# A sparse-attention mixer: the indexer's projections first, relevance on halves of the array, tile 0's sums first

## The reference, cut to what matters

```
def dsa_mixer(h, w_in, cq_g, ckv_g, w_uq, w_uk, w_uv):
    cq, ckv, qi, ki, wi = jnp.split(h @ w_in, C_SPLITS, axis=-1)    # widths 384, 256, 8*64, 64, 8
    q = (rmsnorm(cq, cq_g) @ w_uq).reshape(b, s, C_HEADS, C_NOPE)
    ckv = rmsnorm(ckv, ckv_g)
    q_lat = jnp.einsum('bshd,hcd->bshc', q, w_uk)
    ...
    for i0 in range(0, s, Q_BLOCK):                                 # two tiles of 128 queries
        rel = jax.nn.relu(jnp.einsum('bthd,bsd->bths', qi[:, i0:end], ki[:, :end]))
        score = jnp.einsum('bths,bth->bts', rel, wi[:, i0:end]).astype(jnp.float32)
        _, idx = lax.top_k(jnp.where(admissible, score, -jnp.inf), kk)      # kk = 64
        c_sel = jax.vmap(lambda c, i: c[i])(ckv[:, :end], idx)
        logits = jnp.einsum('bthc,btkc->bthk', q_lat[:, i0:end], c_sel).astype(jnp.float32) * scale
        ...
```

## Time and profile before

| what | value |
|---|---|
| median of three runs | 1085.67 us |
| the profiled execution, its own time | 1085.41 us |
| its span, first to last instruction | 1083.7 us |
| TensorE busy | 1070.7 us, 99% of the span |
| DVE busy, ACT busy | 776.0 us (72%), 564.6 us (52%) |
| 748 to 845 us: TensorE, DVE, ACT busy | 96.4, 69.9, 58.8 of 97.0 us |
| granted TensorE clock, mean | 0.999 |
| DMA | 194.59 MB, mean 180 GB/s |

### The profile page before, as it was taken

One profiled execution on the slowest core, in us unless ns is written; L12 is line 12 of the kernel. 1 busy time (PEld: TensorE's weight loads), 2 busy tenths in 40 slices (PEclk: granted clock), 3 DMA queues, 4 the chain that ended last, 5 costly groups with the idle time before them and its releaser, 6 DMA issues.

```text
span 1083.7 us, 16043 instructions
## 1 busy us (share of the span) xinstructions
PE 1070.7 (99%) x6172; PEld 938.9 (87%) x6172; DVE 776.0 (72%) x1015; ACT 564.6 (52%) x816; POOL 67.8 (6%) x169
## 2 busy tenths in 40 slices
PE   8999999999999999999999999999999999999997
PEld 7888888998889888888888888888978989888886
DVE  5966769875886786676778667678487768676675
ACT  6534446667766753443465344345466666443442
POOL 3000010110020200000010000002100101000000
PEclk9999999999999999999999999999999999999999
DMA  8756474564144365644536564453804435745641
GB/s 322 249 192 222 165 273 132 170 205 151 50 184 152 108 247 199 228 166 183 194 108 246 209 233 159 190 194 108 272 14 143 175 117 195 252 159 191 222 165 40
DMA packets 50155, 194.59 MB, mean 180 GB/s; under 512 B 4496, under 2 KB 24480, under 8 KB 31792
## 3 DMA queue, kind: packets, MB, share of 16 engines
q1 hardware_dynamic: 48832, 189.54, 49.2%
q0 software_dynamic: 1264, 4.25, 1.4%
HBM read 192.73 MB, written 1.05 MB: 179 GB/s over the span
## 4 chain that ended last, share of the span: by engine, by line
PE 91%; DVE 5%; ACT 2%; issue 1%; DMA 1%; POOL 0%; SPq 0%; POOLq 0%; ACTq 0%; DVEq 0%
PE psum L960 21%; PE psum L1076 21%; PE psum L968 11%; PE psum L941 5%; PE psum L1061 3%; PE psum L1298 3%; PE psum L946 3%; PE psum L784 2%; PE psum L786 2%; PE psum L785 2%; PE psum L980 1%; PE psum L1267 1%; PE psum L1168 1%; PE psum L810 1%; PE psum L811 1%; PE psum L809 1%
## 5 line engine op out<-in xcount | busy, mean ns | idle before, releaser
L2322 DVE TENSOR_TENSOR w_ring<-raw,w_ring 128x2048 fp32r<-128x2048 f32 (+2 forms) x120 | 272.8, 2273 | 25.4 <-ACT w_ring L1656 25.1
L1656 ACT ACTIVATE w_ring<-raw 128x2048 fp32r<-128x2048 f32 x121 | 230.7, 1907 | 47.3 <-DMA raw<-in_ffn_w_gate 25.3
L2439 DVE TENSOR_REDUCE work<-psum 128x256 f32<-128x512 f32 x172 | 114.4, 687 | 175.3 <-PE psum L968 161.2
L960 PE MATMUL psum<-h_both,w_ring 128*128 128x512 f32 x1024 | 237.3, 389 | 0.0
L960 PEld LDWEIGHTS psum<-h_both,w_ring 128*128 128x128 f32 x1024 | 192.2, 188 | 39.9
L1076 PE MATMUL psum<-w_ring,g_both 128*128 128x512 f32 x936 | 220.0, 390 | 0.0
L1076 PEld LDWEIGHTS psum<-w_ring,g_both 128*128 128x128 f32 x936 | 173.2, 188 | 34.3
L1754 ACT ACTIVATE V<-work 128x512 f32<-128x512 f32 x44 | 27.9, 634 | 249.3 <-DVE work L2448 249.3
L968 PEld LDWEIGHTS psum<-h_both,w_ring 128*128 128x128 f32 x1024 | 127.1, 192 | 2.5
L968 PE MATMUL psum<-h_both,w_ring 128*128 128x256 f32 x1024 | 127.9, 283 | 0.0
L2322 DVE TENSOR_TENSOR w_ring<-QT,w_ring 128x2048 fp32r<-128x2048 f32 x40 | 91.4, 2285 | 2.4 <-ACT w_ring L1656 2.4
(11 more groups left out here) (336 smaller groups left out, 1560.7 us busy)
## 6 DMA issues: line engine op xcount, KB each, us to landing
raw<-in_ffn_w_gate SPq DMA_DIRECT2D x43, 1024.0 KB, 4.8
raw<-in_ffn_w_up SPq DMA_DIRECT2D x43, 1024.0 KB, 4.8
QT<-in_ffn_w_down SPq DMA_DIRECT2D x40, 1024.0 KB, 4.8
raw<-in_ab_w_in SPq DMA_DIRECT2D x7, 1024.0 KB, 5.5
gain_row<-in_norm_g POOLq DMA_DIRECT2D x8, 512.0 KB, 6.6
raw<-in_ffn_w_down SPq DMA_DIRECT2D x4, 1024.0 KB, 4.7
raw<-in_xa_wk SPq DMA_DIRECT2D x4, 1024.0 KB, 4.8
raw<-in_ab_w_out SPq DMA_DIRECT2D x4, 1024.0 KB, 5.0
```

Of the source, the lines that this page charges most:

```text
L960: nc.tensor.matmul(outs[-1][:, :], hi[:, k, P * j:P * (j + 1)], h_both[:, k].rearrange("p a n -> p (a n)"), start=(k == 0), stop=False)
L1656: nc.scalar.activation(w_hi[:, c % RING, 0:k * n], raw_at(c)[:, 0:k * n], ACT.Copy)\
L2322: nc.vector.tensor_tensor(w_lo[:, c % RING, 0:k * n], raw_at(c)[:, 0:k * n], w_hi[:, c % RING, 0:k * n].bitcast(F32), ALU.subtract).then_i ...
L2439: nc.vector.tensor_reduce(dst[:, p % 2, TOK * j:TOK * (j + 1)], bank(name).rearrange("p (a n) -> p n a", a=2), AX.X, ALU.add)\
```

## The change

Five things change in stage 5, and nothing elsewhere:

1. The chunks are cut and ordered anew: c.2 (the last 128 columns of the query latents, the keys and the head weights), c.0, qi.0, qi.1, and last c.1 (the key-value latents alone). `mixer_begin` takes c.2 and c.0.
2. The keys are scaled into both halves of one row, with no zeros, and two transposes instead of four make one `kiT`, in which both halves of the rows hold the 64 keys. A relevance product takes 64 rows: the head in rows 0 to 63 into one bank, the head in rows 64 to 127 into another. `head_of` gives the head that stands in each place. A call of `relevance(t, m)` on TensorE is four products for two banks.
3. c.1 is projected tile by tile between the relevance products, and its copies and squares follow on ACT.
4. Tile 0's four sums come before tile 1's. DVE does five of tile 0's eight rounds, two of tile 1's sums, the scaling of the key-value latents, the last three rounds, the mask, and two sums more.
5. queries(1) stands before cckvT's transposes and keys(0), instead of after keys(0).

```diff
-C_COLS = [("c.0", (0, 256)), ("c.1", (256, 512)), ("c.2", (512, 640), (1152, 1224)), ("qi.0", (640, 896)),
-          ("qi.1", (896, 1152))]
+C_COLS = [("c.2", (256, 384), (1152, 1224)), ("c.0", (0, 256)), ("qi.0", (640, 896)), ("qi.1", (896, 1152)),
+          ("c.1", (384, 640))]
...
+def head_of(i, j):
+
+    return 4 * (i // 2) + i % 2 + 2 * j
+
+
+RELEVANCE = [(t, i) for t in range(NT) for i in range(4)]
...
-    rel0.0 rel0.1 rel1.0 rel1.1 ccqT.0 ccqT.1 cckvT rel0.2 rel0.3 cuq.0.0 rel1.2 rel1.3 cuk.0 cuq.0.1
+    rel0.0 rel0.1 c.1.0 rel0.2 rel0.3 c.1.1 rel1.0 rel1.1 ccqT.0 ccqT.1 cuq.0.0 rel1.2 rel1.3 cuq.0.1 cckvT cuk.0
...
-LAST_USE = {"ua": "mk.1", "uqn": "uqn.1", "ukv": "v.1", "ca": "cuq.1.1", "cb": "cuv.1.1"}
+LAST_USE = {"c.1": "c.1.1", "ua": "mk.1", "uqn": "uqn.1", "ukv": "v.1", "ca": "cuq.1.1", "cb": "cuv.1.1"}
...
-            mixer_begin(5, ["c.0", "c.1"])
-            token_major("c.2", h_hi, h_lo)
+            mixer_begin(5, ["c.2", "c.0"])
+            pe.wait_ge(ki_done, 1)
+            transposes("kiT", [kk2[:, t, 0:P] for t in range(NT)])
             feature_major("qi.0", h_hi, h_lo)
-            pe.wait_ge(ki_done, 1)
-            transposes("kiT", [kk2[:, t, P * j:P * (j + 1)] for j in range(2) for t in range(NT)])
-
-            def relevance(t, i):
+
+            def relevance(t, m):
                 n = P * (t + 1)
-                up(f"rel{t}.{i}", [(slice(TOK * j, TOK * j + n),
-                                    [(qiT[:, i, P * t:P * (t + 1)], kiT[:, j, 0:n])]) for j in range(2)])
+                outs = [take(f"rel{t}.{2 * m + j}") for j in range(2)]
+                for i in range(2):
+                    for j in range(2):
+                        o = slice(64 * j, 64 * (j + 1))
+                        last = nc.tensor.matmul(outs[j][:, TOK * i:TOK * i + n], qiT[o, 2 * m + i, P * t:P * (t + 1)],
+                                                kiT[o, 0, 0:n], start=True, stop=True)
+                        if i:
+                            filled(f"rel{t}.{2 * m + j}", last)
...
             relevance(0, 0)
+            filled("qi.1", feature_terms(out_[:, TOK:2 * TOK], hi, lo, h_hi, h_lo, 1))
+
+            def key_value_latent(t):
+                hi, lo = weights(C["c.1"])
+                filled(f"c.1.{t}", token_terms(take(f"c.1.{t}")[:, 0:256], hi, lo, h_hi, h_lo, t))
+
+            key_value_latent(0)
+            ready("qi.1")
             relevance(0, 1)
-            filled("qi.1", feature_terms(out_[:, TOK:2 * TOK], hi, lo, h_hi, h_lo, 1))
+            key_value_latent(1)
             relevance(1, 0)
-            relevance(1, 1)
             pe.wait_ge(lat_done, 3)
             transposes("ccqT.0", [lat[:, t, P * k:P * (k + 1)] for k in (0, 1) for t in range(NT)])
             transposes("ccqT.1", [lat[:, t, P * 2:P * 3] for t in range(NT)])
-            pe.wait_ge(lat_done, 4)
-            transposes("cckvT", [lat[:, t, QL + P * k:QL + P * (k + 1)] for k in (0, 1) for t in range(NT)])
...
-            relevance(0, 2)
-            relevance(0, 3)
             ready("ccqT.0")
             ready("ccqT.1")
             queries(0)
-            relevance(1, 2)
-            relevance(1, 3)
+            relevance(1, 1)
+            queries(1)
+            pe.wait_ge(lat_done, 4)
+            transposes("cckvT", [lat[:, t, QL + P * k:QL + P * (k + 1)] for k in (0, 1) for t in range(NT)])
             ready("cckvT")
             keys(0)
-            queries(1)
             sparse_scores(0)
...
-            for i in range(2):
-                split_to(C[f"c.{i}"] + 2)
-                evacuate(f"c.{i}", lat[:, :, 256 * i:256 * (i + 1)],
-                         bank(f"c.{i}").rearrange("p (t n) -> p t n", t=NT))
-            split_to(C["c.2"] + 2)
-            act.wait_ge(*freed["c.1"])
+            split_to(C["qi.1"])
+            evacuate("c.0", lat[:, :, 0:256], bank("c.0").rearrange("p (t n) -> p t n", t=NT))
+            act.wait_ge(*freed["c.0"])
             act.wait_ge(*freed["c.2"])
-            for name, a, b in (("ccq", 0, QL), ("cckv", QL, QL + KVL)):
-                for t in range(NT):
-                    square(name, t, lat[:, t, a:b])
+            for t in range(NT):
+                square("ccq", t, lat[:, t, 0:QL])
+            split_to(C["c.1"])
+
+            def key_value_latent(t):
+                evacuate(f"c.1.{t}", lat[:, t, QL:QL + KVL], bank(f"c.1.{t}")[:, 0:KVL])
+                act.wait_ge(*freed[f"c.1.{t}"])
+                square("cckv", t, lat[:, t, QL:QL + KVL])
...
+            evacuate("kiT", kiT[:, 0, :], bank("kiT")[:, 0:TOK])
             indexer(0)
-            evacuate("kiT", kiT[:, :, :].rearrange("p h n -> p (h n)"))
             relevance(0, 0)
             relevance(0, 1)
             indexer(1)
+            key_value_latent(0)
+            relevance(0, 2)
+            relevance(0, 3)
+            key_value_latent(1)
             relevance(1, 0)
             relevance(1, 1)
...
+            latent_rows("ccqT.0", 0, 2)
+            latent_rows("ccqT.1", 2, 1)
...
-            relevance(0, 2)
-            relevance(0, 3)
             queries(0)
             relevance(1, 2)
             relevance(1, 3)
+            queries(1)
+            latent_rows("cckvT", 3, 2)
             keys(0)
             split_to(C["co.0"])
-            queries(1)
             keys(1)
...
-            for i in range(3):
-                split_to(C[f"c.{i}"] + 2)
-
+            split_to(C["qi.0"])
             dve.wait_ge(*full("c.2"))
             b = bank("c.2").rearrange("p (t n) -> p t n", t=NT)
-            nc.vector.tensor_copy(lat[:, :, 512:640], b[:, :, 0:128])
-            nc.vector.memset(kk2[:, :, 64:192], 0.0)
+            nc.vector.tensor_copy(lat[:, :, 256:384], b[:, :, 0:128])
             n = norm_no["pre5"]
             for t in range(NT):
                 dve.wait_ge(rstd_done[t], n + 1)
-                for o in (0, 192):
+                for o in (0, 64):
...
+            split_to(C["qi.1"])
+            latent("ccq", 0, QL)
+            split_to(C["c.1"])
...
-            for t, i in RELEVANCE:
-                relevance(t, i)
-            top_rounds(0, range(rounds))
+            for i in range(4):
+                relevance(0, i)
+            top_rounds(0, range(5))
+            relevance(1, 0)
+            relevance(1, 1)
+            latent("cckv", QL, QL + KVL)
+            top_rounds(0, range(5, rounds))
             top_mask(0)
+            relevance(1, 2)
+            relevance(1, 3)
```

More of the change, by code:

```diff
@@ L186, in bank_uses @@
     fill(5)
-    names("c.0 c.1 c.2 qi.0 kiT qi.1")
+    names("c.2 c.0 kiT qi.0 qi.1")
     out.extend(SPARSE.format(*units_of("dsa")).split())
@@ L2045, in _, with latent_rows @@
             ffn(4)
-            for i in range(2):
-                split_to(C[f"c.{i}"] + 2)
-                evacuate(f"c.{i}", lat[:, :, 256 * i:256 * (i + 1)],
-                         bank(f"c.{i}").rearrange("p (t n) -> p t n", t=NT))
-            split_to(C["c.2"] + 2)
-            act.wait_ge(*freed["c.1"])
-            act.wait_ge(*freed["c.2"])
-            for name, a, b in (("ccq", 0, QL), ("cckv", QL, QL + KVL)):
-                for t in range(NT):
-                    square(name, t, lat[:, t, a:b])
+            split_to(C["qi.1"])
+            evacuate("c.0", lat[:, :, 0:256], bank("c.0").rearrange("p (t n) -> p t n", t=NT))
+            act.wait_ge(*freed["c.0"])
+            act.wait_ge(*freed["c.2"])
+            for t in range(NT):
[5 more added lines that the diff above has]
+                square("cckv", t, lat[:, t, QL:QL + KVL])
+            def latent_rows(name, k, n):
+                act.wait_ge(*full(name))
+                for j in range(n):
+                    ins = nc.scalar.activation(latT[:, k + j, :], bank(name)[:, TOK * j:TOK * (j + 1)], ACT.Copy,
+                                               scale=pcol[:, CCQ + k + j:CCQ + k + j + 1])
+                ins.then_inc(freed[name][0], 1)
             def indexer(i):
@@ L2072, in _ @@
             indexer(1)
+            key_value_latent(0)
+            relevance(0, 2)
+            relevance(0, 3)
+            key_value_latent(1)
             relevance(1, 0)
             relevance(1, 1)
-            for name, k in (("ccqT.0", 0), ("ccqT.1", 2), ("cckvT", 3)):
-                n = 1 if name == "ccqT.1" else 2
-                act.wait_ge(*full(name))
-                for j in range(n):
-                    ins = nc.scalar.activation(latT[:, k + j, :], bank(name)[:, TOK * j:TOK * (j + 1)], ACT.Copy,
-                                               scale=pcol[:, CCQ + k + j:CCQ + k + j + 1])
-                ins.then_inc(freed[name][0], 1)
+            latent_rows("ccqT.0", 0, 2)
+            latent_rows("ccqT.1", 2, 1)
             def queries(p):
@@ L2744, in _, with latent @@
             dve.wait_ge(ki_done, 1)
-            for name, a, b in (("ccq", 0, QL), ("cckv", QL, QL + KVL)):
+            def latent(name, a, b):
                 for t in range(NT):
```

10 lines of the change are left out of this document (4 added, 6 removed).

## The result

| kernel | median, us | runs | against the kernel before |
|---|---|---|---|
| before | 1085.78 | 20 | |
| changed | 1087.92 | 20 | 1.0021, 95% interval 1.0014 to 1.0028 |
| changed, second comparison | 1087.55 | 11 | 1.0007, 0.9998 to 1.0016 |
| changed, third comparison | 1087.82 | 11 | 1.0022, 1.0012 to 1.0031 |

The forecast was 1087.3. The first result lies 0.6 us above it and inside its range of 1086.1 to 1088.2. By the three ratios together, weighted by their intervals, the changed kernel is 1.0017 of the one before, 1.8 us slower. The forecast was 1.65 us.

What follows compares the result with a forecast made beforehand. TensorE, 91% of the span, was taken as the bound. The stage's +0.10 us and 1.55 us of switches made +1.65; on the profiled 1085.41 that is 1087.06, and 0.26 to the median gave 1087.3, range 1086.1 to 1088.2.

Steps and rivals of the forecast that it cites:

- Level start: Start of the stage: the shorter first chunk's 0.2 us is lost and the next chunk still starts at 752.02 us.
- Row halves: Relevance products: opposite halves of the array overlap fully, blocks take 0.43 and 0.86 us, and 2.6 us go.
- Rival A: Relevance blocks: the halves take turns without overlap, 2.6 us more, +4.2 in all, 1089.9 us; chance 0.13.
- rival B: Relevance blocks: records start in strict order, five slots instead of four, 0.65 us more, 1088.0 us; chance 0.10.
- Switches: Four relevance blocks: each pays one entry into and one exit from the row-half mode, 1.8 us added.
- e + x: Switch cost at a relevance block: entry e of 0.20 us (between 0 and 0.39) plus exit x of 0.25 us.
- Rival D: Relevance blocks: switches cost nothing, so +0.1 to +0.4 us, about 1085.9 us, no change; chance 0.10.
- Three waits: TensorE idles for ACT's copies before queries(0), keys(0) and the first scores: 1.5, 1.1 and 0.9 us, 3.5 added.
- After this point: From the first probability transposes on: both orders are alike, TensorE stays dense, and nothing takes the lag back.
- DVE: Tile 0's sums end near 779 us and its mask near 788; two TensorE waits on DVE go, 0.7 us.
- rival C: First relevance block: the fifth chunk (c.1) comes late, block 1.9 us late, +3.6, 1089.3 us; chance 0.05.
- E: Faster: switches free and the three waits only a third as long, -2.2 us, 1083.4 us; chance 0.06.

Runs made afterwards that it cites:

- e4: The changed kernel with both products of the lower row half ahead of both of the upper one in each relevance block; 1087.56 us, ratio 1.0016.
- e2: The changed kernel with zero-padded relevance products over all 128 rows instead of row halves; 1088.64 us, ratio 1.0027.
- e3: The changed kernel with the same TensorE products reordered so that other work covers all three handoffs; 1084.11 and 1083.94 us, ratios 0.9987 and 0.9985.
- e6: e1 with the four transposes of the first query latents put ahead of the first tile 1 block; 1085.77 us, ratio 0.9996.
- e7: e3 with whole-height zero-padded relevance products instead of row halves; 1085.68 us, ratio 0.9995.
- e1: The kernel before with only the relevance products on row halves (one form of the keys, two transposes); 1086.67 us, ratio 1.0010.

## Why the prediction was right

| step | before | forecast | after, less 0.47 |
|---|---|---|---|
| key transposes | | 760.55 | 760.53 |
| third block | | 779.8 | 779.78 |
| queries(0) | | 783.3 | 783.28 |
| keys(0) | | 791.3 | 791.38 |
| first probability transposes | 799.22 | 800.87 | 801.11 |

- **Level start**: right. The first chunk's 0.2 us is lost at the transposes of x; the next chunk stands at 752.02.
- **Row halves**: full overlap, 2.6 us, as taken. Rival A is refuted by the block lengths (1.07 and 0.64 us, where turns would take 1.72 and 0.87 and the switches on top), rival B by the same lengths and by e4.
- **Switches**: e + x was put at 0.45 us. From the rows: the last product before a block starts at 769.74 and the block would be due at 769.86, so the block is 0.09 late. From its start to the next product are 0.64, 0.21 over the four slots. The product after that comes 0.22 later, 0.10 over its pitch. That is 0.40 for both. The tile 1 blocks take 1.07, also 0.21 over. That this is the halves' and not the place's is shown by e2: its whole-height blocks, at the same places behind the same work, start on pitch, take 0.81 and 1.73 us and are followed on pitch. Rival D is refuted. The forecast of 1.55 us for the four blocks was about 0.15 too high.
- **Three waits**: 1.5, 1.1 and 0.9 were forecast; 1.56, 0.98 and 0.73 are marked. The forecast counts by pitch, and a bracket begins only at the end of the last record, which is later. By pitch the first is 781.32 + 0.65 to 783.75 = 1.78, the second 790.27 + 0.44 to 791.85 = 1.14, the third 791.85 + 1.72 to 794.58 = 1.01 us: 3.9 in sum where 3.5 was forecast. The first is the longer because TensorE was done sooner, the switch being cheaper than forecast. ACT's copies set its end, and from the block's start to queries(0) are 3.50 us against 3.47 forecast. So the forecast had the switches too dear and the waits too short, and the two partly cancel. With a few hundredths at keys(0) and in the products behind, the last row of the table is 0.24 later than forecast.
- **After this point**: right, as far as the traces can tell. I had written that nothing takes the lag back. Between the two traces 1.89 becomes 1.67, but that is mostly the 0.17 us stretch at 828.10, which in e3 comes and goes with the execution. Nor does being later decide it: counted from 739 us, e6 reaches that place level with the kernel before (within 0.02 us) and e7 0.2 us sooner, and neither has the stop. So 1.67 against 1.65 is nearer than the forecast deserves: it was 0.24 short at the last row of the table, and one stop in one trace of the kernel before hides most of that.
- **DVE**: tile 0's sums ended at 779.45 and its mask was written at 787.83 (less the 0.47: 778.98 and 787.36; forecast: near 779 and near 788). The losses of 0.44 and 0.28 us in the earlier trace rows are gone, and TensorE had nothing more to gain from it.
- **c.1's chunk (rival C)**: its ACT part started at 764.76, where 764.1 and the 0.47 make 764.6. The block was not late.
- **E**: the handoffs are not shorter than taken.

Timeline of DVE, changed kernel, the mask of tile 0:

```profile
779.49 0.29 DVE L2788 MAX8 top<-vaug 128x8 f32<-128x128 f32 x1
...
787.83 0.23 DVE L2793 TENSOR_SCALAR xmT<-vaug 128x128 f32<-128x128 f32 x1
```

Change or no change: the forecast called 0.2% the edge and gave 0.60 to "no change" and 0.35 to slower. The first result, 1.0021 with 1.0014 to 1.0028 around it, lies on that edge, so which side it fell on is luck. The miss of size is 0.6 us in the time, of which about 0.15 is the stage's (1.8 by the three ratios in place of 1.65) and 0.1 the kernel before (1085.78 for 1085.67). The rest is within the scatter of a comparison: 1.0007 to 1.0022 for one kernel.

One cost the prediction never looked at: a block asks for both its banks before its first product. In the changed kernel other work stands ahead of each block (24 to 72 products, or queries(0)), its banks were free, and this had no price. In e1 it cost 1.37 us. That the prediction wasn't hurt by it was not its doing.

## What to carry to other kernels

Before moving a piece away from between two others, write down which copy it covered. Here three handoffs TensorE to ACT to TensorE, each about 0.2 us and the copies queued on ACT, left TensorE idle for 3.3 us when uncovered, more than the 2.6 us of array time saved. Once work stood over them again, the same savings made the kernel 0.14% faster than before. Packing products onto row halves also makes one block ask for two banks at the same time: count when the second bank comes free, not only the first.

## What the runs showed of the hardware

- Products of 64 rows on opposite row halves run side by side in full: eight fp32 records of 256 columns in four slots of 0.215 us, and the starts of a pair are 7 ns apart (13 ns where both products of one half come first in the program). The order in the program within the block doesn't matter for this (e4).
- Going from whole-height products to row halves and back costs 0.35 to 0.40 us for both ways together, in blocks of 0.64 and of 1.07 us. Whole-height blocks at the same places (e2) have no such cost.
- Ahead of a wait for ACT's copies, a shorter block brings less than it saves. e2's block at 780.83 is 0.66 us longer than the changed kernel's at 780.25, but from the block's start to queries(0) are 3.78 us against 3.50, only 0.28 more.
- The start of the stage moves from execution to execution by over 4 us with the same program ahead of it (-0.6 to +4.1 us at 739 us), while what the stage itself takes repeats within 0.1 us for the changed kernel (1.67, 1.77, 1.68) and within 0.16 for e3, where the stop at the values makes the difference. A change of 1 us is read from the stage, not from the span.
